# RWKV mixer in a two-layer network: the receptance is multiplied with its exponential on GpSimd, and the backward decays compute the keys' exponential first

## What is computed

```python
def _rwkv7_scan(S0, r, w, k, v, kk, a):
    def step(S, inp):
        r_t, w_t, k_t, v_t, kk_t, a_t = inp
        sa = jnp.einsum('bhvk,bhk->bhv', S, kk_t)
        S = (S * w_t[:, :, None, :] - sa[..., None] * (kk_t * a_t)[:, :, None, :]
             + v_t[..., None] * k_t[:, :, None, :])
        return S, jnp.einsum('bhvk,bhk->bhv', S, r_t)
...
        kk = hd(k * k_k)
        kk = kk / jnp.maximum(jnp.sqrt(jnp.sum(kk * kk, axis=-1, keepdims=True)), 1e-12)
        k = k * (1.0 + (a - 1.0) * k_a)
...
    yf_c, Sf_c = _rwkv7_scan(S0, r_c, wf_c, k_c, v_c, kk_c, a_c)
    yb_c, Sb_c = _rwkv7_scan(S0, *_flip_seq(r_c, wb_c, k_c, v_c, kk_c, a_c))
```

## Time and profile before

| what | value |
|---|---|
| median of 3 runs | 1971.7 us (1970.67 to 1972.4) |
| the profiled execution, its own time | 1971.56 us |
| its span, first to last instruction | 1969.7 us |
| mean granted TensorE clock | 0.971 of full speed |
| busy in the span: PE, PEld, DVE, ACT, POOL | 93%, 81%, 63%, 43%, 16% |

### The profile page before, as it was taken

The page is one execution under the profiler, slowest core; times in us unless marked ns, Lnnn a source line. Parts: engine busy times, 40 slices in busy tenths (PEclk is TensorE's granted clock), DMA queues, the critical chain, the costliest instruction groups (busy, mean ns, idle before and its releaser), DMA issues. The chain is left out here.

```text
span 1969.7 us, 42687 instructions
## 1 busy us (share of the span) xinstructions
PE 1833.7 (93%) x18256; PEld 1604.7 (81%) x18256; DVE 1240.9 (63%) x2163; ACT 850.8 (43%) x1561; POOL 318.0 (16%) x361
## 2 busy tenths in 40 slices
PE   7999877968999999999999799999889999889997
PEld 5787436858688888888878699999689999789997
DVE  4574886676656424533766778745868656767753
ACT  4321566354423212222437345534744355554432
POOL 0201205335140000013002121012040012030001
PEclk9999988979999999999999999999989999999998
DMA  9752940020522323232420366555145465226552
GB/s 329 206 181 80 306 150 3 2 66 2 172 86 87 106 86 107 86 98 74 150 64 1 100 194 180 190 179 167 44 150 183 140 195 190 87 87 209 177 162 95
DMA packets 248982, 254.68 MB, mean 129 GB/s; under 512 B 6914, under 2 KB 247187, under 8 KB 248691
## 3 DMA queue, kind: packets, MB, share of 16 engines
q1 hardware_dynamic: 239214, 242.86, 38.7%
q10 hardware_dynamic: 8740, 8.51, 1.3%
q0 software_dynamic: 864, 0.98, 0.3%
HBM read 251.29 MB, written 1.05 MB: 128 GB/s over the span
## 5 line engine op out<-in xcount | busy, mean ns | idle before, releaser
L578 DVE TENSOR_TENSOR RING_rounded<-RING,SC_rounded 128x1024 fp32r<-128x1024 f32 (+2 forms) x390 | 460.0, 1222 | 234.8 <-ACT SC_rounded L571 234.4
L598 PE MATMUL bank<-OT_rounded,SC_rounded 128*128 128x256 f32 (+1 forms) x1808 | 575.8, 318 | 15.6 <-DVE HT_rounded L1173 6.8
L600 PE MATMUL bank<-OT_rounded,RING_rounded 128*128 128x256 f32 (+1 forms) x1808 | 571.7, 316 | 0.0
L599 PE MATMUL bank<-HT_rounded,SC_rounded 128*128 128x256 f32 (+1 forms) x1808 | 570.7, 316 | 0.0
L571 ACT ACTIVATE SC_rounded<-RING 128x1024 fp32r<-128x1024 f32 (+2 forms) x390 | 374.0, 1010 | 358.9 <-DMA RING<-in_l_mlp_w 182.6
L598 PEld LDWEIGHTS bank<-OT_rounded,SC_rounded 128*128 128x128 f32 x1808 | 344.4, 191 | 44.8 <-issue 8.8
L600 PEld LDWEIGHTS bank<-OT_rounded,RING_rounded 128*128 128x128 f32 x1808 | 343.0, 190 | 23.8
L599 PEld LDWEIGHTS bank<-HT_rounded,SC_rounded 128*128 128x128 f32 x1808 | 343.0, 190 | 23.3
L598 PE MATMUL bank<-PT_rounded,SC_rounded 128*128 128x256 f32 (+1 forms) x896 | 277.2, 309 | 5.5 <-DVE RING_rounded L578 5.5
L600 PE MATMUL bank<-PT_rounded,RING_rounded 128*128 128x256 f32 (+1 forms) x896 | 277.2, 309 | 0.0
L599 PE MATMUL bank<-PT_rounded,SC_rounded 128*128 128x256 f32 (+1 forms) x896 | 276.8, 309 | 0.0
(11 more groups left out here) (574 smaller groups left out, 2777.0 us busy)
## 6 DMA issues: line engine op xcount, KB each, us to landing
RING<-in_l_mlp_w SPq DMA_DIRECT2D x64, 1024.0 KB, 5.5
RING<-in_w_ffn_in SPq DMA_DIRECT2D x44, 1024.0 KB, 5.1
RING<-in_l_mod_w SPq DMA_DIRECT2D x32, 1024.0 KB, 6.6
RING<-in_l_w_in SPq DMA_DIRECT2D x25, 1024.0 KB, 6.0
RING<-in_w_ffn_out SPq DMA_DIRECT2D x16, 768.0 KB, 4.9
RING<-in_w_in SPq DMA_DIRECT2D x10, 1024.0 KB, 5.5
RING<-in_w_ffn_out SPq DMA_DIRECT2D x16, 640.0 KB, 4.6
PT<-in_l_mod_w SPq DMA_DIRECT2D x8, 1024.0 KB, 10.1
```

Source lines behind the costliest of these rows:

```text
L578: net.nc.vector.tensor_tensor(low, whole, net.high4(s, m)[:, 0:self.w.kts[s], :].bitcast(F32), ALU.subtract).then_inc(self.split_ready, 1)
L598: net.nc.tensor.matmul(bank[:, tokens], high, x_high, start=start, stop=False)
L599: net.nc.tensor.matmul(bank[:, tokens], high, x_low, start=False, stop=False)
L600: return net.nc.tensor.matmul(bank[:, tokens], low, x_high, start=False, stop=stop)
```

## The change

In the preparation the multiplication of the receptance with its exponential leaves VectorE's list, and GpSimd gets it as four instructions of 512 columns, one for each t, when the first exponential is there. VectorE waits for them (`received`) ahead of the biases, the last thing that it does in the stage. In the backward decays the same is done, and the two exponentials change places on ScalarE: `bd`, which the keys need, comes first, so that VectorE waits for one exponential instead of two, and GpSimd waits for the second.

```diff
@@ rwkv_prepare_stage @@
-        turned, rate_used = st.sem("turned"), st.sem("rate_used")
+        turned, rate_used, received = st.sem("turned"), st.sem("rate_used"), st.sem("received")
...
+        @st.gpsimd
+        def _(pool):
+            pool.wait_ge(exped, 1)
+            for t in range(4):
+                receptance = mem.kr[:, t, :, 1, :]
+                pool.tensor_tensor(receptance, receptance, mem.r[:, t], ALU.mult).then_inc(received, 1)
...
             link(nc.vector.tensor_tensor(flat(mem.b), flat(mem.b), flat(mem.kk), ALU.mult))
-            dve.wait_ge(exped, 1)
-            nc.vector.tensor_tensor(kr[:, :, 1, :], kr[:, :, 1, :], flat(mem.r), ALU.mult)
             dve.wait_ge(exped, 2)
...
+            dve.wait_ge(received, 4)
             mod.biases(dve)
@@ rwkv_back_decay_stage @@
             act.wait_ge(cum_ready, 1)
+            act.activation(flat(mem.bd), flat(mem.cum), ACT.Exp, scale=DECAY).then_inc(exped, 1)
             act.activation(kr[:, :, 1, :], flat(mem.cum), ACT.Exp, scale=-DECAY).then_inc(exped, 1)
-            act.activation(flat(mem.bd), flat(mem.cum), ACT.Exp, scale=DECAY).then_inc(exped, 1)
             act.wait_ge(cum_ready, 2)
...
+        @st.gpsimd
+        def _(pool):
+            pool.wait_ge(exped, 2)
+            for t in range(4):
+                receptance = mem.kr[:, t, :, 1, :]
+                pool.tensor_tensor(receptance, receptance, mem.r[:, t], ALU.mult).then_inc(received, 1)
...
-            dve.wait_ge(exped, 2)
-            nc.vector.tensor_tensor(kr[:, :, 1, :], kr[:, :, 1, :], flat(mem.r), ALU.mult)
+            dve.wait_ge(exped, 1)
             link(nc.vector.tensor_tensor(flat(mem.kd), flat(mem.bd), flat(mem.k), ALU.mult))
             nc.vector.tensor_tensor(flat(mem.bd), flat(mem.bd), flat(mem.b), ALU.mult)
             dve.wait_ge(exped, 3)
             nc.vector.tensor_tensor(kr[:, :, 0, :], kr[:, :, 0, :], flat(mem.kk), ALU.mult)
+            dve.wait_ge(received, 4)
             mod.biases(dve)
```

More of the change, by code:

```diff
@@ L3159, in rwkv_back_decay_stage @@
                                                 st.sem("exped"), st.sem("dve_own"))
-        carry_ready = st.sem("carry_ready")
+        carry_ready, received = st.sem("carry_ready"), st.sem("received")
         @st.sync
```

## The result

The change makes the kernel slower: 1978.78 us in the median of 10 runs (1973.94 to 1985.4) against 1972.05 us for ten runs of the kernel before. The ratio is 1.0035, with a 95% interval from 1.0023 to 1.0048, or 4.5 to 9.5 us. The forecast was 1977.0 us, +5.4.

A forecast was written before the change was run, and what follows sets the result against it. TensorE is busy 93% of the time, but in the two changed stages VectorE and ScalarE set the end. +4.2 us (preparation) and +1.2 (backward decays) make +5.4 on 1971.56: 1977.0 us, range 1974.8 to 1979.0.

The forecast's parts named there:

- The path: Preparation: VectorE up to L3136, then ScalarE to the end; the moved multiplication, 2.21 us, is off it and worth 0.
- Turns at 1.06 us: Preparation: each of four GpSimd multiplications delays VectorE by 1.06 us ahead of L3136, so the stage ends 4.2 us later.
- The 0.84 of the broadcast case: Lower price per GpSimd instruction, from L3877 beside L3773: 3.4 + 0.1 = 3.5 us, 1975.1 us in all; chance 0.15.
- Which instructions pay: Preparation: nine VectorE instructions with two SBUF inputs stand ahead of L3136; GpSimd gets all four through in turns with them.
- Backward decays: Exchange removes a 0.93 us wait, but turns and the wait for GpSimd's last instruction make the stage end 1.2 us later.
- the forecast's own range: Whole kernel: 1975.8 to 1978.2 us, for turns of 1.0 to 1.15 us and 0.4 of the recurrences; chance 0.60.
- whole turns: Rival, both stages: each GpSimd instruction costs VectorE its full 1.28 us; 5.1 + 1.9 = 7.0, 1978.6 us; chance 0.08.
- the outer range: Whole kernel: 1974.8 to 1979.0 us, covering turns of 1.06, 0.84 and 1.28 us with 0.4 beyond.
- The recurrences: Two recurrence stages, same instructions, 90.5 and 90.9 us: a shifted start may move a stage by some 0.4 us either way.
- the preparation is 48 us long: Sign expected in the profile after: the preparation stage, 44.0 us before, lasts 48 us.
- No exclusion: Rival: GpSimd works beside VectorE; preparation unchanged, backward decays 3.1 us earlier, 1968.5 us; chance 0.07.
- GpSimd comes last: Rival: GpSimd gets its turn only after L3143; preparation pays 0, backward decays 1.2 us, 1972.8 us; chance 0.06.

The follow-up runs named there:

- e1: The change in the preparation only, backward decays as in the kernel before: preparation 26.62 us against 22.31; timed ratio 1.0025 to the kernel before.
- e3: The changed preparation with GpSimd's four multiplications also waiting for rate_used, backward decays of before: preparation 23.40 us against 22.31 before; timed ratio 1.0014.
- e7: The changed preparation with four extra GpSimd multiplications, backward decays of before: preparation 30.57 us against 26.60 with the change; not timed.
- e5: The change with GpSimd's multiplications replaced by fills that read nothing: preparation 22.37 us, backward decays 9.46 us; not timed.
- e8: Preparation of before; backward decays of the change with most of the exponentials VectorE uses written to PSUM: 9.90 us against 12.68 before; timed ratio 1.0002.
- e4: The kernel before with only the two exponentials exchanged in the backward decays, receptance kept on VectorE: 11.67 us against 12.68; timed ratio 0.9999.
- e2: The change in the backward decays only, preparation as in the kernel before: backward decays 13.93 us against 12.68; timed ratio 1.0012.

## Why the prediction was right

- *The path.* VectorE up to the keys by the rate, then ScalarE to the end: ScalarE's idle time went from 4.09 to 8.32 us, forecast 8.3, and its row behind is unchanged. Moving L3139 gained nothing in the preparation, as written. Shown by e1 and e3.
- *Turns at 1.06 us.* Forecast +4.2 us in the preparation from four turns at 1.06; measured +4.29, and 0.99 for each further one in e7. The 0.84 of the broadcast case and the 1.28 of the whole instruction were both farther off. The rule cited from the Trainium skill, "SBUF — State Buffer", section "Who interferes with whom", agrees in what it says of inputs: two of VectorE's in SBUF against a GpSimd instruction that reads (the change), not against one that only writes (e5), and not with one of VectorE's inputs in PSUM (e8). The other half of what was cited, that whichever starts first has the shared ports for the whole instruction, the Trainium skill states for two SBUF inputs in another section of that page, "SBUF: two separate sides". It is close, but by the lengths in the profile somewhat too much: VectorE loses 1.0 to 1.07 us by a GpSimd instruction that takes 1.28.
- *Which instructions pay.* I had let GpSimd alternate with nine VectorE instructions one by one. In the rows three of the four turns fell to the small subtractions, where two of VectorE's slip between two turns, and only one to L3141. The sum is the same, since all four come ahead of the rate.
- *Backward decays.* Forecast +1.2 us, measured +1.24; L3221 and L3223 stretched by 0.94 and 1.06 us, the last wait 2.37 us for a forecast of 2.3. e4 shows the exchange's part (-1.0), e2 the whole (+1.25).
- *The whole.* +5.4 forecast; the stages sum to +5.5, and the timed runs give +6.9 with an interval from 4.5 to 9.5. The time alone would not have decided: 1978.78 us lies above the forecast's own range (1975.8 to 1978.2), and 0.2 us from the 1978.6 of "whole turns". What decides against that rival is the lengths of the stages: it has +5.1 and +1.9, measured are +4.29 and +1.24. That the time fell inside the outer range (up to 1979.0) is in part luck, since where the timed runs lost 1.4 us more than the two stages is not shown.
- *The recurrences.* From the first matmul of the forward one to that of the next stage it was 91.5 us before, 90.4 after and 89.7 to 91.5 in the experiments; of the backward one 91.2, 92.1 and 90.0 to 91.1. That is up to 2 us, more than the 0.4 that I had allowed. The prediction had no term for the clock ahead of L2977 either, and so the sign "the preparation is 48 us long" failed: it was 46.0 us in the profile after (44.3 before).
- *Rivals.* "No exclusion" was worked out at -3.1 us for the backward decays; e5 measures -3.2 where there is none. "GpSimd comes last" is out by the rows after; forced by e3 it would still have cost 1.1 us in the preparation, a term that the prediction's version of it lacked.

## What to carry to other kernels

Before work goes from VectorE to GpSimd, look at what VectorE does at that moment: if its instructions have two SBUF inputs, GpSimd's reads are paid by VectorE one after the other, at 1.0 to 1.07 us for each multiplication of 512 columns here, also by instructions of four columns, and the price falls on whatever path these stand on, though the moved work was off it. Place such work behind the instruction that others wait for (e3: that took 3.2 of the 4.3 us away, and the stage was still 1.1 longer than with the work left on VectorE), or put one of VectorE's inputs in PSUM, which made the two truly parallel here. Where runs spread by ten microseconds, measure a stage between two fixed instructions: here the unchanged ones repeated to 0.02 us.

## What was not expected of the hardware

- Instructions of 4 and 16 columns pay a full turn: 1.26 us in place of 0.17 for the first subtraction.
- GpSimd's price on VectorE went with the length of its own instruction, less 0.2 us: 1.07 of 1.28 us with two full inputs, 0.84 of 1.04 with one of them a broadcast, 0.40 of 0.61 for a copy. Fills, which read nothing, take 0.53 us and cost nothing.
- The clock granted to TensorE in the same stretch of the same work differs from run to run, and with it the first part of the preparation: the same eight matmuls took 3.70 to 6.22 us, which is half of the effect studied here.
